# Transposed factors of six triangular inverses: from products and adds to block transposes

## Reference

```python
lhs = jnp.where(strict, jnp.einsum('zbhnid,zbhnjd->zbhnij', kb, k) * decay, 0.0) + jnp.eye(C)
u_base = lax.linalg.triangular_solve(lhs, v * beta[..., None], left_side=True, lower=True, unit_diagonal=True)
```

## Time and profile before

| | before |
|---|---|
| median of three runs | 2038.7 us |
| profiled execution, span | 2039.0 us |
| PE busy | 1853.9 us (91%) |
| PEld busy | 1540.7 us (76%) |
| DVE busy | 1283.6 us (63%) |
| ACT busy | 965.0 us (47%) |
| POOL busy | 130.2 us (6%) |
| L1636 PE | 576 instructions, 86.9 us |
| L1645 PE | 576 instructions, 106.0 us |
| L1648 PE | 480 instructions, 95.5 us |
| L1135 and L1138 DVE | 72 and 60 instructions, 30.6 and 24.9 us |
| L603 POOL | 72 instructions, 90.9 us |

### The profile page before, as it was taken

The page is one execution under the profiler, slowest core; times in us unless marked ns, Lnnn a source line. Parts: engine busy times, 40 slices in busy tenths (PEclk is TensorE's granted clock), DMA queues, the critical chain, the costliest instruction groups (busy, mean ns, idle before and its releaser), DMA issues.

```text
span 2039.0 us, 24409 instructions
## 1 busy us (share of the span) xinstructions
PE 1853.9 (91%) x9616; PEld 1540.7 (76%) x9616; DVE 1283.6 (63%) x1278; ACT 965.0 (47%) x867; POOL 130.2 (6%) x132
## 2 busy tenths in 40 slices
PE   4995499996999899768799999999999999999998
PEld 2674488983899888667478888788887888888886
DVE  6426423224444306453288888888888888888886
ACT  1142221121443322221177676776776767767674
POOL 1000233230000000331000000000000000000000
PEclk9985599897999989878899999999999999999999
DMA  5440000001456524100289999899999999999993
GB/s 185 131 139 0 0 1 1 1 1 49 155 171 203 187 83 143 64 1 1 103 314 372 330 359 373 317 376 322 370 352 336 373 325 371 345 343 371 325 374 144
DMA packets 202076, 428.90 MB, mean 210 GB/s; under 512 B 13440, under 2 KB 37268, under 8 KB 202004
## 3 DMA queue, kind: packets, MB, share of 16 engines
q1 hardware_dynamic: 202004, 427.90, 58.6%
HBM read 426.82 MB, written 1.05 MB: 210 GB/s over the span
## 4 chain that ended last, share of the span: by engine, by line
PE 88%; DVE 7%; ACT 2%; POOL 1%; issue 1%; DMA 0%; DVEq 0%; SPq 0%; POOLq 0%; ACTq 0%
PE bank L1945 15%; PE bank L1947 15%; PE bank L1946 15%; PE bank L1822 4%; PE bank L1636 4%; PE bank L1645 3%; PE bank L1754 3%; PE bank L1755 3%; PE bank L1756 3%; PE bank L1648 3%; PE bank L1733 2%; PE bank L1508 2%; PE bank L1519 2%; PE bank L1954 2%; PE bank L1964 1%; PE bank L1988 1%
## 5 line engine op out<-in xcount | busy, mean ns | idle before, releaser
L1455 DVE TENSOR_TENSOR split<-ring,split 128x2048 fp32r<-128x2048 f32 x336 | 764.5, 2289 | 128.4 <-ACT split L895 125.9
L895 ACT ACTIVATE split<-ring 128x2048 fp32r<-128x2048 f32 x336 | 638.5, 1919 | 180.7 <-PE bank L1947 176.1
L1945 PE MATMUL bank<-split 128*128 128x512 f32 x896 | 354.8, 396 | 2.6 <-DVE split L1432 1.4
L1947 PE MATMUL bank<-split 128*128 128x512 f32 x896 | 349.8, 390 | 0.0
L1946 PE MATMUL bank<-split 128*128 128x512 f32 x896 | 349.1, 390 | 0.0
L1945 PEld LDWEIGHTS bank<-split 128*128 128x128 f32 x896 | 168.4, 188 | 36.0 <-issue 1.6
L1947 PEld LDWEIGHTS bank<-split 128*128 128x128 f32 x896 | 168.3, 188 | 35.8
L1946 PEld LDWEIGHTS bank<-split 128*128 128x128 f32 x896 | 168.6, 188 | 33.3
L1945 PE MATMUL bank<-split,ehr_ 128*128 128x512 f32 x448 | 180.2, 402 | 0.0
L1947 PE MATMUL bank<-split,ehr_ 128*128 128x512 f32 x448 | 175.0, 391 | 0.0
L1946 PE MATMUL bank<-split,ehr_ 128*128 128x512 f32 x448 | 174.7, 390 | 0.0
(11 more groups left out here) (413 smaller groups left out, 2565.0 us busy)
## 6 DMA issues: line engine op xcount, KB each, us to landing
ring<-in_od_moe_gate SPq DMA_DIRECT2D x112, 1024.0 KB, 7.1
ring<-in_od_moe_up SPq DMA_DIRECT2D x112, 1024.0 KB, 7.3
ring<-in_od_moe_down SPq DMA_DIRECT2D x112, 1024.0 KB, 6.8
ring<-in_od_w_in SPq DMA_DIRECT2D x7, 2048.0 KB, 8.1
ring<-in_ev_w_in SPq DMA_DIRECT2D x6, 2048.0 KB, 8.1
ring<-in_ev_ffn_gate SPq DMA_DIRECT2D x11, 1024.0 KB, 5.4
ring<-in_ev_ffn_up SPq DMA_DIRECT2D x11, 1024.0 KB, 8.0
ring<-in_ev_ffn_down SPq DMA_DIRECT2D x5, 2048.0 KB, 7.7
```

What stands on the lines that cost most here:

```text
L895: act.activation(wst[:, r % NSTAGE, 0, :], ring[:, (r % NHALF) * HALF:(r % NHALF + 1) * HALF], ACT.Copy).then_inc(w_hi, 1)
L1455: dve.tensor_tensor(wst[:, r % NSTAGE, 1, :], ring[:, (r % NHALF) * HALF:(r % NHALF + 1) * HALF], wst[:, r % NSTAGE, 0, :].bitcast(F32), S ...
L1945: pe.matmul(o, hi, wh, start=start, stop=False)
L1947: return pe.matmul(o, lo, wh, start=False, stop=stop)
```

## The change

In levels 1 to 4 the update of P is no longer multiplied. Only T is updated (X as stationary operand, half of T's columns moving), VectorE adds it, and then transposes T into P in 32x32 blocks; T's blocks are at most 32 wide after these levels, so that this is the whole transpose. P's start, too, is such a transpose of T on VectorE, and TensorE's transposes and ScalarE's copies of them are gone. In level 5 (`MID`) both updates are still multiplied, T's only in the 64x64 corner that level 6 needs, with 32 columns, and the two products of one matrix stand one behind the other, T's first. In level 6 (`TOP`) X and the update of P are 64x64x64 products, and VectorE copies the result where it added before.

```diff
+        MID, TOP = NLEV - 2, NLEV - 1
+        def inv_half(z):
+            near, far = slice(0, 64), slice(64, P)
+            return (near, far, slice(0, 32)) if z == 0 else (far, near, slice(96, P))
...
             def inv_copies(p):
-                for g in range(2):
-                    act.wait_ge(p0_ps, 2 * p + g + 1)
-                    act.activation(Pm[g], B[2 + g][:, :].rearrange("p (u s) -> p u s", u=4),
-                                   ACT.Copy).then_inc(p0_sb, 1)
...
-                            act.activation(odd_even(Xm[g], lev, odd)[:, :, 0, :], packed(B[g], lev, 0)[:, :, 0, :],
+                            own, other, _ = inv_half(INV[p][g][0])
+                            act.activation(Xm[g][own, :, other], packed(B[g], lev, 0)[own, :, 0, :],
                                            ACT.Copy).then_inc(x_cp, 1)
...
             def inv_adds(p):
+                flat4 = "p u s -> p (u s)"
+                for g in range(2):
+                    dve.wait_ge(t0_rdy, 2 * p + g + 1)
+                    dve.transpose(Pm[g].rearrange(flat4), Tm[g].rearrange(flat4)).then_inc(p0_sb, 1)
...
-                        pv = odd_even(Pm[g], lev, odd)
-                        last = dve.tensor_tensor(pv, packed(B[2 + g], lev, 0), pv, ADD)
-                        if lev < NLEV - 1:
+                        if lev < MID:
                             tv = odd_even(Tm[g], lev, not odd)
-                            last = dve.tensor_tensor(tv, packed(B[2 + g], lev, 64), tv, ADD)
+                            link(dve.tensor_tensor(tv, packed(B[2 + g], lev, 0), tv, ADD))
+                            last = dve.transpose(Pm[g].rearrange(flat4), Tm[g].rearrange(flat4))
+                        elif lev == MID:
+                            own, _, near = inv_half(z)
+                            tv = Tm[g][own, :, near]
+                            dve.tensor_tensor(tv, packed(B[2 + g], lev, 64)[own, :, 0, :], tv, ADD)
+                            pv = odd_even(Pm[g], lev, odd)
+                            last = dve.tensor_tensor(pv, packed(B[2 + g], lev, 0), pv, ADD)
+                        else:
+                            own, other, _ = inv_half(z)
+                            last = dve.tensor_copy(Pm[g][own, :, other], packed(B[2 + g], lev, 0)[own, :, 0, :])
...
             def invert(p):
-                for g in range(2):
-                    pe.wait_ge(t0_rdy, 2 * p + g + 1)
-                    for u in range(4):
-                        last = pe.transpose(B[2 + g][:, P * u:P * u + P], Tm[g][:, u, :], ident[:, :])
-                    last.then_inc(p0_ps, 1)
...
                         for u in range(4):
-                            if lev < NLEV - 1:
-                                o, i = B[g][:, P * u:P * u + P], Pm[g][:, u, :]
+                            if lev < TOP:
+                                last = pe.matmul(B[g][:, P * u:P * u + P], Am[g][:, u, :], Pm[g][:, u, :],
+                                                 start=True, stop=True)
                             else:
-                                o, i = B[g][:, P * u:P * u + 64], pm[:, u, 0, :]
-                            last = pe.matmul(o, Am[g][:, u, :], i, start=True, stop=True)
+                                last = pe.matmul(B[g][own, P * u:P * u + 64], Am[g][other, u, own], Pm[g][other, u, other],
+                                                 start=True, stop=True)
...
                         for u in range(4):
-                            last = pe.matmul(packed(B[2 + g], lev, 0)[:, u], Tm[g][:, u, :], xm[:, u],
-                                             start=True, stop=True)
-                            if lev < NLEV - 1:
-                                last = pe.matmul(packed(B[2 + g], lev, 64)[:, u], Xm[g][:, u, :], tm[:, u],
-                                                 start=True, stop=True)
+                            if lev < MID:
+                                last = pe.matmul(packed(B[2 + g], lev, 0)[:, u], Xm[g][:, u, :],
+                                                 odd_even(Tm[g], lev, not odd)[:, u], start=True, stop=True)
+                            elif lev == MID:
+                                pe.matmul(packed(B[2 + g], lev, 64)[own, u, 0, :], Xm[g][own, u, own],
+                                          Tm[g][own, u, near], start=True, stop=True)
+                                last = pe.matmul(packed(B[2 + g], lev, 0)[:, u], Tm[g][:, u, :],
+                                                 odd_even(Xm[g], lev, odd)[:, u], start=True, stop=True)
+                            else:
+                                last = pe.matmul(packed(B[2 + g], lev, 0)[own, u, 0, :], Tm[g][own, u, own],
+                                                 Xm[g][own, u, other], start=True, stop=True)
```

More of the change, by code:

```diff
@@ L330, in hybrid_trunk @@
         t0_rdy = sem("t0_rdy")
-        p0_ps = sem("p0_ps")
         p0_sb = sem("p0_sb")
@@ L709, in inv_copies @@
             def inv_copies(p):
-                Pm, Xm = INVB[p][1], INVB[p][2]
-                for g in range(2):
-                    act.wait_ge(p0_ps, 2 * p + g + 1)
-                    act.activation(Pm[g], B[2 + g][:, :].rearrange("p (u s) -> p u s", u=4),
-                                   ACT.Copy).then_inc(p0_sb, 1)
+                Xm = INVB[p][2]
                 for lev in range(1, NLEV):
@@ L1629, in invert @@
                         pe.wait_ge(am_rdy, n)
-                        pm = odd_even(Pm[g], lev, odd)
+                        own, other, _ = inv_half(INV[p][g][0])
                         for u in range(4):
-                            if lev < NLEV - 1:
-                                o, i = B[g][:, P * u:P * u + P], Pm[g][:, u, :]
-                            else:
-                                o, i = B[g][:, P * u:P * u + 64], pm[:, u, 0, :]
-                            last = pe.matmul(o, Am[g][:, u, :], i, start=True, stop=True)
+                            if lev < TOP:
+                                last = pe.matmul(B[g][:, P * u:P * u + P], Am[g][:, u, :], Pm[g][:, u, :],
+                                                 start=True, stop=True)
+                            else:
+                                last = pe.matmul(B[g][own, P * u:P * u + 64], Am[g][other, u, own], Pm[g][other, u, other],
+                                                 start=True, stop=True)
@@ L1637, in invert @@
                         last.then_inc(x_ps, 1)
                     for g in range(2):
-                        n = inv_seq(p, lev, g)
-                        odd = INV[p][g][0] == 0
-                        pe.wait_ge(x_cp, n)
-                        xm = odd_even(Xm[g], lev, odd)
-                        tm = odd_even(Tm[g], lev, not odd)
-                        for u in range(4):
-                            last = pe.matmul(packed(B[2 + g], lev, 0)[:, u], Tm[g][:, u, :], xm[:, u],
-                                             start=True, stop=True)
-                            if lev < NLEV - 1:
-                                last = pe.matmul(packed(B[2 + g], lev, 64)[:, u], Xm[g][:, u, :], tm[:, u],
-                                                 start=True, stop=True)
+                        z = INV[p][g][0]
@@ new lines, in invert @@
+                        odd = z == 0
+                        pe.wait_ge(x_cp, inv_seq(p, lev, g))
+                        own, other, near = inv_half(z)
+                        for u in range(4):
+                            if lev < MID:
[9 more added lines that the diff above has]
+                                                 Xm[g][own, u, other], start=True, stop=True)
```

5 lines of the change are left out of this document (2 added, 3 removed).

## The result

The changed kernel takes 2058.7 us (median of four runs, 2055.29 to 2063.5) where the kernel before takes 2038.5 (2032.76 to 2043.74): a ratio of 1.0093, 95% interval 1.0073 to 1.0112. It is **slower** by 20 us; forecast was 12 us faster. The profiled execution is the slowest of the four (2063.5), so its rows lie some 5 us above the median.

The account below looks back on a forecast made before the run. TensorE was taken as the bound, busy 91% of 2039.0 us. Gains of 27 (levels 1 to 4), 6 (level 6) and 3 (after idle), less 11 (level 5) and 13 (clock), gave 12 us: 2027 us, range 2015 to 2037.

Parts of the forecast that it names:

- What bounds the kernel, levels 1 to 4: TensorE bounds; in levels 1 to 4 a level takes 4.4 us for 5.53, gaining 27 us in six passes.
- Rival D: Levels 1 to 4: VectorE becomes the bound with a transpose of 1.63 us, giving 2061 us; chance 0.07.
- E: Levels 1 to 4: latencies make a level 4.9 us, the clock takes the rest, 2039 us; chance 0.05.
- Level 5's work: Level 5's second products: 16 tile changes at 0.17 us make 5.4 us for 3.52, losing 11 us in six passes.
- Rival A: Level 5: changes of tile cost nothing, it gains 5 us instead of losing 11, giving 1998 us; chance 0.15.
- Level 6's work: Level 6: 64x64x64 products take 2.7 us for 3.75, gaining 6 us in six passes.
- After the idle: Start of each pass at 1.2 GHz: more wide products among the instructions, counted as 3 us gain over all passes.
- The clock: Level 5: few columns bring a clock fall in three of six passes at 4.3 us on average, costing 13 us.
- rival C: Clock falls in level 5 every pass and stays down through narrow products: 44 us, 2058 us; chance 0.25.
- The prediction's own sign of being wrong: Wrong if a tile change costs under 0.05 us or over 0.3, or the clock does the same in all six passes.

Follow-up runs that it names:

- the kernel with the wide dummies: Changed kernel plus unused 256-column products, one behind each matrix of level 5 and two ahead of level 6's second products: 2045.2 us.
- both with dummies in level 6: Changed kernel with level 5 as before it, plus dummies ahead of level 6's second products: two of 256 columns 2014.4 us, four of 32 columns 2044.2 us.
- Feeding that stretch: Changed kernel with levels 5 and 6 as before it, plus eight unused 256-column products ahead of each pass: 2008.2 us.
- levels 1 to 4 alone: Changed kernel with the products, copies and adds of levels 5 and 6 as before the change: 2017.9 us.
- level 6 alone: Kernel before the change with only level 6's 64x64x64 products and the start by DVE's transposes from the change: 2049.6 us.
- whole-array level 5: Changed kernel with level 6 as before it and level 5's T update by whole-array weights, still 32 columns moving: 2056.2 us.
- the kernel fed in both places: Changed kernel with old level 5, plus 256-column dummies: eight ahead of each pass, two ahead of level 6's second products: 2007.8 us.
- both kernels with a thin level 6 and an old level 5: Level 6 as in the change, level 5 as before: with the change's levels 1 to 4 2035.6 us, with the old ones 2049.6 us.

## Why the prediction was wrong, point by point

**What bounds the kernel, levels 1 to 4.** Right. 4.31 us a level for 4.4 forecast, with the two holes of PE. The transpose, priced between 0.43 and 1.63 and taken at 0.69, has 0.711 in the group of its line, and PE waits for it 22 times, 6.9 us in all:

```profile
L1144 DVE STREAM_TRANSPOSE arena<-arena 128x512 f32<-128x512 f32 x48 | 34.1, 711 | 1.7
```

Rival D falls, and with 4.31 for 4.9 us a level E does. By the warm level, (5.53 - 4.31) x 24 = 29 us; by the medians the part brings 21. That the first levels of a pass run partly at 1.2 GHz is one reason; how much of the 8 us it explains, no run shows.

**Level 5's work.** Right in kind, too dear in size: 0.59 us per matrix at 2.4 GHz, of which a full product takes 0.22 and a small one 0.13 (level 6's 16 half-width loads take 1.0 us in the kernel with the wide dummies). The rest, 0.24, is two changes of tile, 0.12 each for 0.17. The Trainium skill (TensorEngine Tiling, Key Properties) says that such a change drains TensorE. The trace agrees, by these 0.12 us. The phase takes 4.7 instead of 5.4 us, +7 us in six passes for +11. Rival A falls: a change isn't free.

**Level 6's work.** Right: 2.66 us for 2.7 forecast.

**After the idle.** Not borne out. In the first pass of the profiled executions the changed kernel has its clock back at 256 us, the old one at 249, and levels 1 and 2 take 11.9 us together (247.14 to 259.08), where they took 12.0 (247.10 to 259.14): nothing of their 2.4 us was gained. But kernels with the same code up to there had it back at 248 (both with dummies in level 6), 253 and 254, so one execution does not give the term its sign. Over all passes 3 us of gain were counted. Feeding that stretch, instead, gave 10.

**The clock.** The step that failed. The place was named rightly (level 5, in the form of rival C), but the term was "a fall in three of six passes at 4.3 us", 13 us. It fell in level 5 of six passes out of six, and costs 40 to 43 us by the medians: some 10 us in each RWKV pass and 1 to 2 in each of DeltaNet, by the table. Rival C's 44, in its own split of 10 and 2, and its 2058 us, are what was measured. Two readings of the earlier trace rows should have carried more weight. The fall at 1003.4, with PE and PEld 100% busy at 8 columns, says that being busy is no cover; the score stretches, on which the hold was rested, have 128 and 256 columns, and level 5's have 32 and 64. And what stands behind level 5 in RWKV is level 6, R and U, 64 columns each, and in the earlier trace rows the clock did not come back through 6.7 us of 64-column products either: here it stayed down for 20 us. "Three of six at 4.3 us" was too low in both factors: too few passes, and less than half of the price of an RWKV pass. The prediction's own sign of being wrong, the clock doing the same in all six passes, is what came.
The second thing not seen: level 6 is thin enough by itself, in front of the same R and U. That its smaller products are cheap was counted, what they do to the clock was not. With the work alone, -29 + 7 - 6.5, the change would stand at 2010; by the runs, at 2016 (the one with dummies) to 2018 (levels 1 to 4 alone, plus 0.5).

What stays open: why level 6 alone tips the clock in two passes and not in the other two, why whole-array level 5 tips it in three and not in the second, and why it fell in the fourth pass of the kernel fed in both places, behind an old level 5. The spread of 20 to 30 us in the runs of both kernels with a thin level 6 and an old level 5 has no cause shown either; that in each execution another number of passes loses the clock would fit, and only one execution of each was profiled.

## What to carry to other kernels

In this kernel a product made smaller was only cheaper where what followed kept its clock. So before shrinking operands in a stretch of TensorE, look at the columns of the stretch and of what stands behind it, and price a fall as the duration of all narrow work behind it once more, in every repetition of the code. Keep the part that removes instructions (one product replaced by VectorE's block transpose: 21 us here), leave the part that makes them thin. Where TensorE has to wait or runs thin products, a wide dummy product into an unused bank can be worth its time several times over: two of them a pass, 6 us in six, took 21 us off, and eight in an idle wait 10 us; thin dummies of the same duration did nothing.

## What the runs showed of the hardware

The granted clock fell from 2.4 to 1.2 GHz in a stretch with TensorE busy for 3.15 of 3.15 us, and stayed at 1.2 for 20 us in which it was busy throughout (273.1 to 293.6). Halving the columns of every second product in a phase of 3.6 us, with neither time nor instruction count changed, brought such falls in three of four RWKV passes and 38 us. Two dummy products of 256 columns between level 6's products kept the clock (2014.4 us), four of 32 columns in the same time did not (2044.2). A block transpose of 128x512 fp32 takes VectorE 0.711 us, about as much as most of its arithmetic of that size (0.68 to 0.69); 64-column weights load at 0.065 us each, against 0.11 for 128 columns; a change between a 64x64 tile and the whole array costs 0.12 us at 2.4 GHz.
